# A two-block transformer kernel on one core: the compression's first layer turned round, its scores by alternating heads, and matmuls of zeros at the start

## The reference, cut to what matters

```
def compress(t, pos, w1, w2):
    c = kv(t).reshape(B, G, S // 16, 16, Dh)                # G = 2 groups, Dh = 64
    blocks = concatenate([c[:, :, :-1], c[:, :, 1:]], axis=3)
    blocks = (blocks + pos).reshape(B, G, 15, 32 * Dh)      # 15 blocks of 2048 numbers
    return gelu(blocks @ w1) @ w2                           # w1 2048 x 128, w2 128 x 64
kc = compress(k_cmp, ...); vc = compress(v_cmp, ...)
s_c = einsum('bghtd,bgnd->bghtn', q, kc) * scale + bias     # 8 heads x 256 tokens x 15 blocks
o_c = einsum('bghtn,bgnd->bghtd', masked_softmax(s_c), vc)
```

## Time and profile before

| | |
|---|---|
| median of 3 runs (lowest, highest) | 1478.65 us (1478.64, 1479.38) |
| the profiled execution: its time, its span | 1484.34 us, 1482.5 us |
| PE busy | 1405.8 us, 95% of the span |
| PE's idle time named by the list of waits | DVE a_lo 14.4, DVE w_lo 13.7, DVE x 9.2, DVE res 8.3 us, ... |
| chain that ended last | PE 81%, DVE 10%, ACT 4% |

### The profile page before, as it was taken

The page is one execution under the profiler, slowest core; times in us unless marked ns, Lnnn a source line. Parts: engine busy times, 40 slices in busy tenths (PEclk is TensorE's granted clock), DMA queues, the critical chain, the costliest instruction groups (busy, mean ns, idle before and its releaser), DMA issues.

```text
span 1482.5 us, 24445 instructions
## 1 busy us (share of the span) xinstructions
PE 1405.8 (95%) x9990; PEld 1308.6 (88%) x9990; DVE 973.8 (66%) x1660; ACT 696.7 (47%) x1143; POOL 84.9 (6%) x78
## 2 busy tenths in 40 slices
PE   7998989999998998999998999899999999999997
PEld 7997779999898976899997999789998899889996
DVE  4664675555759557655557586687777655687777
ACT  4745344343376533434333555455554544454453
POOL 0321000000005000000000002040000000000000
PEclk9998999999999988999998999999999999999999
DMA  8733045454453212655544333345544534345541
GB/s 308 254 143 114 30 146 195 172 193 177 142 227 115 90 53 86 227 172 193 177 171 138 132 115 125 132 166 193 187 183 171 185 115 143 131 168 198 200 171 57
DMA packets 38343, 233.22 MB, mean 157 GB/s; under 512 B 4984, under 2 KB 8776, under 8 KB 11864
## 3 DMA queue, kind: packets, MB, share of 16 engines
q1 hardware_dynamic: 36168, 224.18, 42.4%
q0 software_dynamic: 2064, 7.47, 1.6%
HBM read 230.55 MB, written 1.09 MB: 156 GB/s over the span
## 4 chain that ended last, share of the span: by engine, by line
PE 81%; DVE 10%; ACT 4%; issue 2%; DMA 1%; POOL 1%; SPq 0%; DVEq 0%; ACTq 0%
PE bank L741 24%; PE bank L742 23%; PE bank L743 23%; DVE w_lo L577 2%; PE bank L841 2%; PE bank L912 1%; ACT w_hi L567 1%; PE bank L851 1%; PE bank L934 1%; PE bank L936 1%; PE bank L935 1%; DVE a_lo L598 1%; DVE nstat L1525 1%; DMA arena<-in_w_idx 1%; PE bank L873 1%
## 5 line engine op out<-in xcount | busy, mean ns | idle before, releaser
L577 DVE TENSOR_TENSOR w_lo<-raw,w_hi 128x1024 fp32r<-128x1024 f32 x404 | 482.6, 1232 | 102.7 <-ACT w_hi L567 99.5
L741 PE MATMUL bank<-a_hi,w_hi 128*128 128x256 f32 x1856 | 530.4, 286 | 4.4 <-DVE w_lo L577 4.4
L742 PE MATMUL bank<-a_lo,w_hi 128*128 128x256 f32 x1856 | 526.1, 283 | 0.0
L743 PE MATMUL bank<-a_hi,w_lo 128*128 128x256 f32 x1856 | 526.0, 283 | 0.0
L567 ACT ACTIVATE w_hi<-raw 128x1024 fp32r<-128x1024 f32 x404 | 406.2, 1050 | 93.9 <-PE bank L743 89.4
L741 PEld LDWEIGHTS bank<-a_hi,w_hi 128*128 128x128 f32 x1856 | 356.7, 192 | 9.4 <-issue 6.0
L742 PEld LDWEIGHTS bank<-a_lo,w_hi 128*128 128x128 f32 x1856 | 357.0, 192 | 1.2
L743 PEld LDWEIGHTS bank<-a_hi,w_lo 128*128 128x128 f32 x1856 | 356.9, 192 | 0.0
L741 PE MATMUL bank<-w_hi,a_hi 128*128 128x256 f32 (+1 forms) x512 | 172.3, 336 | 23.8 <-DVE a_lo L598 14.4
L742 PE MATMUL bank<-w_lo,a_hi 128*128 128x256 f32 (+1 forms) x512 | 165.3, 323 | 0.0
L743 PE MATMUL bank<-w_hi,a_lo 128*128 128x256 f32 (+1 forms) x512 | 164.7, 322 | 0.0
(11 more groups left out here) (242 smaller groups left out, 1491.4 us busy)
## 6 DMA issues: line engine op xcount, KB each, us to landing
raw<-in_stream SPq DMA_DIRECT2D x201, 1024.0 KB, 4.9
bias_t<-bias_rows SPq DMA_DIRECT2D x6, 512.0 KB, 7.9
heads_buf<-in_w SPq DMA_DIRECT2D x2, 1024.0 KB, 8.0
gains<-in_w SPq DMA_DIRECT2D x2, 1024.0 KB, 10.1
gains<-in_ln_g POOLq DMA_DIRECT2D x4, 512.0 KB, 4.7
gains<-in_ln_b POOLq DMA_DIRECT2D x4, 512.0 KB, 6.3
gains<-in_rms_g POOLq DMA_DIRECT2D x3, 512.0 KB, 3.8
res<-in_xT SPq DMA_DIRECT2D x4, 256.0 KB, 5.0
```

The lines of the kernel that those rows point to most:

```text
L577: dve.tensor_tensor(w_lo[:, i % PARTS, half_tile(h)], raw[:, i % SLOTS, half_tile(h)], w_hi[:, i % PARTS, half_tile(h)].bitcast(F32), ALU. ...
L741: pe.matmul(out, lh, rh, start=first, stop=False)
L742: pe.matmul(out, lh, rl, start=False, stop=False)
L743: return pe.matmul(out, ll, rh, start=False, stop=last)
```

## The change

1. The inner layer is turned round: the 30 columns of the blocks are the weights, the 128 columns of w1 move, and keys and values alternate, keys into partitions 0 to 29 of the bank and values into 32 to 61. It is done in four pieces of 8 products instead of two of 16. The result stands in rows, so ACT copies it to `hid_rows`, PE transposes it (key `hidT`), and only then comes gelu; the second layer (`kcv`) moves behind `("S", 1)` and the mixer's read-out.
2. The compressed scores of the even and odd heads alternate product by product, into two banks, in one step.
3. Before its first real product PE does 7 products of zeros, 128 x 128 by 128 x 512, fp32, into the bank that the real ones then overwrite; it waits for POOL's first memset only.

```
+HID_PARTS = 4
+WARM = 7
-        levels += ([("level", 6), ("hid", 0, 0), ("hid", 0, 1), ("b", "hg1"), ("level", 7), ("a", "vsvw"), ("silu",)]
-                   + [("level", 8), ("hid", 1, 0), ("hid", 1, 1), ("phase", "heads"), ("ho", 0), ("ho", 1)])
-        return woven(lead + levels + [("b", "vsvw"), ("kcv",), ("gtT",), ("S", 0), ("a", "nq1"), ("S", 1), ("ho_out",)]
-                     + [("b", "nq1"), ("T", 0), ("phase", "out"), ("S", 2), ("oT", 0), ("oT", 1), ("out", 0, 0, 0)]
+        levels += ([("level", 6), ("hid", 0), ("b", "hg1"), ("level", 7), ("hid", 1), ("a", "vsvw"), ("silu",)]
+                   + [("level", 8), ("hid", 2), ("phase", "heads"), ("ho", 0), ("ho", 1)])
+        return woven(lead + levels + [("b", "vsvw"), ("hid", 3), ("gtT",), ("S", 0), ("hidT",), ("a", "nq1"), ("S", 1), ("ho_out",)]
+                     + [("kcv",), ("b", "nq1"), ("T", 0), ("phase", "out"), ("S", 2), ("oT", 0), ("oT", 1), ("out", 0, 0, 0)]
...
                 b = open_bank((0, "hi0"))
+                pe.wait_ge(zeroed, 1)
+                for _ in range(WARM):
+                    pe.matmul(b[:, 0:512], s_hg[:, 0:P], s_hg[:, 0:512], start=True, stop=True)
...
+            def compress(l, part):
+                b = open_bank((l, "hid")) if part == 0 else bank_of((l, "hid"))
+                wait_drained(pe, (l, "kcvc"))
+                pe.wait_ge(w1k_in, 16 * (l + 1))
+                pe.wait_ge(w1v_in, 16 * (l + 1))
+                for k in range(part * CMP_KT // HID_PARTS, (part + 1) * CMP_KT // HID_PARTS):
+                    for i in range(2):
+                        mm = pe.matmul(b[32 * i:32 * i + 30, 0:P], blk[i][:, k, :, :].rearrange("p g n -> p (g n)"),
+                                       w1[i][:, k, :], start=(k == 0), stop=(k == CMP_KT - 1))
+                if part == HID_PARTS - 1:
+                    close_bank(mm)
+            def turn_hidden(l):
+                wait_drained(pe, (l, "hid"))
+                pe.wait_ge(consts_in, CONSTS)
+                b = open_bank((l, "hidT"))
+                close_bank(pe.transpose(b[:, 0:62], hid_rows[0:62, :], ident[0:62, 0:62]))
...
-                b = open_bank((l, "cs", odd))
-                lo = DH * odd
+                banks = [open_bank((l, "cs", odd)) for odd in range(2)]
                 for tt in range(NT):
                     for j in range(4):
                         c = (tt * 4 + j) * NCP
-                        mm = pe.matmul(b[:, c:c + NC], nq[lo:lo + DH, j, tt * P:(tt + 1) * P],
-                                       kc2[lo:lo + DH, j // 2, :], start=True, stop=True)
+                        mms = [pe.matmul(b[:, c:c + NC], nq[lo:lo + DH, j, tt * P:(tt + 1) * P],
+                                         kc2[lo:lo + DH, j // 2, :], start=True, stop=True)
+                               for b, lo in zip(banks, (0, DH))]
...
+            def hidden_rows(l):
+                key = (l, "hid")
+                wait_full(act, key)
+                for i in range(2):
+                    rows = slice(32 * i, 32 * i + 30)
+                    ins = act.activation(hid_rows[rows, :], bank_of(key)[rows, 0:P], ACT.Copy)
+                ins.then_inc(*drained(key))
...
             pool.memset(cp[:, :, :, :], 0.0).then_inc(zeroed, 1)
+            pool.memset(hid_rows[:, :], 0.0)
```

More of the change, by code:

```diff
@@ L192, in plan_uses @@
         elif kind == "hid":
-            if step[1:] == ((1, 1) if closing else (0, 0)):
+            if step[1] == (HID_PARTS - 1 if closing else 0):
                 uses.append(((l, "hid"), "X"))
+        elif kind == "cs":
+            uses += [((l, "cs", odd), "X") for odd in range(2)]
         elif kind in ("S", "T", "I"):
@@ L199, in plan_uses @@
                 uses.append(((l, "V", step[1] // 2), "V"))
-        elif kind in ("kcv", "gt", "gtT", "cT", "kw", "kwT", "kiT"):
+        elif kind in ("hidT", "kcv", "gt", "gtT", "cT", "kw", "kwT", "kiT"):
             uses.append(((l, kind), "X"))
-        elif kind in ("cs", "co", "ho", "oT"):
+        elif kind in ("co", "ho", "oT"):
             uses.append(((l, kind, step[1]), {"oT": "O", "ho": "H"}.get(kind, "X")))
@@ L842, in level @@
                 mm.then_inc(product_done, 1)
[L844 to L855 removed]
+            def compress(l, part):
[11 more added lines that the diff above has]
+                wait_drained(pe, (l, "hid"))
+                pe.wait_ge(consts_in, CONSTS)
+                b = open_bank((l, "hidT"))
+                close_bank(pe.transpose(b[:, 0:62], hid_rows[0:62, :], ident[0:62, 0:62]))
             def compressed(l):
                 b = open_bank((l, "kcv"))
[L859 removed]
+                wait_drained(pe, (l, "hidT"))
                 pe.matmul(b[:, 0:30], w2[:, l, 0:P], hid[:, :], start=True, stop=True)
@@ L862, in compressed, with compressed_scores @@
                                      w2[:, l, P:P + DH], start=True, stop=True))
-            def compressed_scores(l, odd):
+            def compressed_scores(l):
                 wait_drained(pe, (l, "kcv"))
@@ L1096, in _ @@
                     elif kind == "hid":
-                        compress(l, *step[1:])
+                        compress(l, step[1])
+                    elif kind == "hidT":
+                        turn_hidden(l)
                     elif kind == "kcv":
@@ L1388, in _ @@
                         turned_high(act, (l, "oT", step_[1]), mixed_part(l, step_[1])[0])
-                    elif kind == "hid" and step_[1:] == (1, 1):
+                    elif kind == "hid" and step_[1] == HID_PARTS - 1:
+                        hidden_rows(l)
+                    elif kind == "hidT":
                         hidden_out(l)
@@ L1394, in _ @@
                         act.activation(gate_rows, bank_of(key)[0:24, 0:S], ACT.Exp, scale=-1.0).then_inc(*drained(key))
-                    elif kind == "cs" and step_[1] == 1:
+                    elif kind == "cs":
                         act.wait_ge(cmp_logit, l + 1)
@@ L1828, in _ @@
                     elif kind == "cs":
-                        compressed_logits(l, step_[1])
-                        if step_[1] == 1:
-                            compressed_probs(l)
+                        for odd in range(2):
+                            compressed_logits(l, odd)
+                        compressed_probs(l)
                     elif kind == "cT":
```

19 lines of the change are left out of this document (5 added, 14 removed), and 2 rows, old and new, of the table levels.

## The result

| kernel | median us (lowest, highest), executions | mean clock | ratio to before, 95% interval |
|---|---|---|---|
| before, beside the first runs | 1479.02 (1478.64, 1480.93), 4 | 0.972 (86 later ones) | 1 |
| changed | 1465.80 (1464.53, 1467.11), 4 | 0.978 | 0.9902 [0.9876, 0.9929] |
| changed, a second time (below) | 1471.17 (1469.87, 1471.91), 6 | 0.974 | 0.9947 [0.9927, 0.9968] |

The account below looks back on a forecast made before the run. PE, busy 95% of the span, was taken as the bound. Terms -2.3 - 8.1 - 5.0 + 3.2 - 4.6 + 2.4 gave -14.4 us; 12.6 counted against the 1478.65 median gave 1466.0 us, range 1459 to 1474 (its own 1461 to 1470).

Parts of the forecast that it names:

- the 12.6 counted: Whole kernel: 12.6 of the summed 14.4 us gain credited, since the profiled execution was not typical and the clock may differ.
- Zeros, -2.3: Start: zeros bring the clock's rise at about 7 us, so 24 records take 2.9 us, not 5.23; bounds +2.2 and -2.6.
- Inner layer, -8.1 and -5.0: Inner-layer stages of layers 0 and 1: 26.71 and 23.64 us become 18.6, with pieces of 1.05 us running side by side.
- the wait for DVE's pick: Behind the inner layer's third piece: the mixer's output waits 0.5 us for DVE's pick of level 8, formerly hidden by values.
- The stretch behind, +1.6 each: From vsvw's end to first output product, 15.75 us: grows 0.75 on PE plus 0.88 for DVE's read-outs, in each layer.
- So it costs nothing more: Same stretch: ACT's two 1.28 us table loads and 0.44 us gelu add nothing, as DVE's logits are 1.6 us late too.
- second rival: ACT becomes the bound between 119.7 and 135.5 us: +2.5 us per layer, 1471 to 1472 us; chance 0.08.
- Scores, -2.6 and -2.0: Compressed scores to fifth scores of heads: 9.20 and 8.60 us become 6.6, row halves overlapping, then DVE's softmax setting the end.
- Clock, +1.2 each: Behind the scores: the clock falls again, later, over the wide products; +1.2 us on each layer, bounds 0 and 3.4.
- first rival: Inner layer: column groups don't overlap, pieces take 1.9 us, total gain 8.8 us, 1471 us with caution; chance 0.18.
- third: Inner layer: alternating column groups drain the array, a piece takes 4.5 us, eight add 27 us, 1493 us; chance 0.08.
- fourth: Clock falls in the new stages anyway, or zeros run wholly at half clock: up to +7 us, 1473 us; chance 0.08.

Follow-up runs that it names:

- The kernels with the old form: Kernel before with alternating scores alone, 1476.73 us; kernel before with 128 columns of w1 moving instead of 30 in the inner layer, 1476.96 us.
- the eight that were filled: Changed kernel with products of ident by ident ahead of PE's waits, two misplaced fillings put right: 1460.61 us, ratio 0.9853.

## Why the prediction was right, and where it was not

**Sum and time.** 1466.0 was forecast, 1465.80 measured, and 1468.9 is the mean of all ten executions. The gain is 10.5 +- 2.0 us by them rather than the 12.6 counted or the 13.2 first seen: the forecast's closeness to 0.2 us is partly the first draw. It is luck in a second way. Measured in the profiled executions, the terms add up to -2.4 - 7.8 - 4.4 + 1.8 + 1.5 - 2.65 - 2.05 = -16.0 us, without the +2.4 for the clock (below), and the span fell by 19.0: another 3.0 us came where nothing was changed. Both profiled executions were off their kernels' means, before's slow and the changed one's fast. The range 1459 to 1474 holds every execution.

**Zeros, -2.3.** 2.4 us by the trace (the products behind the first 96 start at 22.16 us and had at 24.55), 2.3 at equal clock. The records of zeros come every 0.85 us up to 5.3 and every 0.43 from 6.0 on: the rise came at 5.7 us, not 7.

**Inner layer, -8.1 and -5.0.** The stages took 18.91 and 19.26 us for 18.6, so -7.8 and -4.4 against the profiled execution. A piece takes 0.996 us for 1.05. What was sized too small: a level ahead of a piece takes 1.88 us for 1.78, half a projection 2.97 for 2.88, and the wait for DVE's pick, put at 0.5, is 0.45 us in layer 0 and 0.80 in layer 1. The rule of the Trainium skill that the prediction weighed ("TensorE: Matmul & The Clock Gate", "Part 3: Packing small matmuls") undersold it: its ratio, which it gives for three groups and 512 columns, made a piece 1.3 us, an estimate. Two groups of columns here run at a full factor of two, and the drained array of "TensorEngine Tiling (Array Packing)", section "Key Properties", is bounded by the runs too: a piece with both its changes of mode is 0.12 us over 8 x 0.109.

**Of what the gain is made.** The prediction put 6.8 us of the inner layer's 13.1 down to half clock before. The kernels with the old form confirm the split: 22.02 us at full clock, so 4.7 and 1.6 us were clock. But it took this from one execution at 0.967, below the mean of 0.9717, and took off only 1.8 us for that. On average the inner layer alone brings 4.9 us, 2.5 of them clock.

**The stretch behind, +1.6 each.** It was +1.8 and +1.5. The price held, its reason only in part. "So it costs nothing more", said of ACT's gelu and its two table loads, is the step that failed: in layer 0 their chain was late as well, by about as much as DVE's. There gelu holds kcv, kcv the second half of nq1, and that the third scores, whose logits DVE starts at 121.71 us; DVE itself had been free since 121.43. With kcv moved away DVE waits 0.9 us for those scores, a third of it ACT's and 0.6 us half clock, and the stretch stays at 17.5 us; with gelu moved away too it is 16.35. So the second rival was half true, without its 2.5 us. In layer 1 the banks are mixed in, and ACT's part there stays open. Timelines of ACT and DVE in the changed kernel:

```profile
114.49 1.28 ACT L1333 ACT_TABLE_LOAD   x1
115.78 0.20 ACT L1333 ACTIVATE hid<-bank 128x30 f32<-128x30 f32 x1
115.87 0.33 ACT L1336 ACTIVATE hid_v<-bank 128x60 f32<-128x60 f32 x2
116.22 1.28 ACT L1316 ACT_TABLE_LOAD   x1
```
```profile
118.60 0.17 DVE L1735 COPY kc<-bank 128x30 f32<-128x30 f32 x1
118.69 0.68 DVE L1736 TENSOR_TENSOR res<-bank,head_blocks 128x512 f32<-128x512 f32 x1
```

PE's wait for gelu was priced at 1.7 us and is 1.9. That it was called free missed that the clock can fall behind it.

**Scores, -2.6 and -2.0.** 2.65 and 2.05; 1.89 us for 32 records; fifth scores 6.55 us behind for 6.6. Right, but for PE's wait for DVE, put at some 2 us:

```profile
146.61 0.70 PE L930 MATMUL bank<-arena 64*128 64x256 f32 x4 [0.77 <-DVE heads_buf L1498]
```

**Clock, +1.2 each.** Right that it falls at the scores all the same, 3.4 us in either layer, but the price was wrong: nothing came on top. The fall lies over records that are followed by the wait for DVE, shortened it to 0.8 us, and the stretch's 6.55 us hold it. The wait and the fall had each been reckoned, but not that one hides the other; this term is 2.4 us too slow in all.

**Rivals.** The groups overlap (first rival wrong, and pieces in turn would have cost 0.46 each, not 0.85, since the overlap reaches further); nothing drains (third wrong); the turned stages keep the clock (fourth wrong).

## What to carry to other kernels

Products with few weight columns and few rows of result can share the array if they write different partitions of the bank; turn a product so that the small side is loaded, and let two such alternate. Read the granted clock before crediting a gain: here about half of it was clock, and one profiled execution can be several microseconds from the mean. Where half clock follows a wait of PE for another engine (here 1.9 to 4.8 us), put products into a bank that is about to be overwritten ahead of the wait, count them to end just short of it, and check in the trace that they hit it. When a step is moved, look also at what the dealing of the banks does to the steps behind it.

## What the runs showed of the hardware

- Two fp32 products, 128 rows by 30 columns of weights with 128 moving columns, into partitions 0 to 29 and 32 to 61 of one bank, start 0.01 us apart, and the next two 0.11 us later: the time of one. With four products of one group ahead of four of the other, a record of the later group starts ahead of three of the earlier (90.69 us, keys before values).
- Moving 30 or 128 columns behind a load of 128 costs the same at full clock (22.02 us a stage, both), but only with 30 did the clock fall inside the stage (5 of 6 against 0 of 2, the latter on other numbers).
- The clock falls behind waits of PE: in the changed kernel run again at 117.0, 127.2, 185.3, 390.1, 441.3, 506.1, 567.5, 768.9, 779.2 and 970.3 us, each behind a wait of 1.9 to 4.8 us. Of the eight that were filled none fell. Not each such wait brings it: none fell behind the 1.9 us at 495.0 and the 1.8 us at 1294.1 of the same run, or behind 2.7 us at 982.2 in the kernel before. At the compressed scores it falls in every profile (144.3 and 526.6 in this one), here with no wait of that length ahead. Some stretches follow waits of only 0.8 us between transposes (946.4, 1147.8, 1274.1), and not in every execution.
- Time goes with the mean clock at 11.9 us per 0.01, 0.4 us for each microsecond at half clock, since part of it lies over PE's waits.
